# Five weight buffers for the experts, heavy and light blocks in turn, and the shared down products inside the first block

## What is computed

```python
s = sigmoid(t @ w_router);  sb = s + b_router          # 64 scores a token
... group-limited top 8 of sb -> idx, weights wk       # normalised, times 2.5
gates = sum over the chosen of wk * one_hot(idx, 64)
act    = silu(t @ w_gate_e) * (t @ w_up_e) * gates     # each expert: 1024 -> 256
routed = act @ w_down_e                                # 256 -> 1024
shared = (silu(t @ w_gate_s) * (t @ w_up_s)) @ w_down_s
y = routed + shared
```

## Time and profile before

| | |
|---|---|
| median of the timed runs | 1057.35 us |
| profiled execution, time and span | 1053.31 us, 1051.5 us |
| TensorE busy | 886.6 us (84%) |
| VectorE, ScalarE, GpSimd busy | 32%, 24%, 15% |
| DMA: bytes moved, mean rate | 299.57 MB, 285 GB/s |
| landing of a gate, up, down load, median | 11.4, 23.2, 22.4 us |
| TensorE waiting for gate/up weights at L1342 | 88.3 us |

### The profile page before, as it was taken

How to read it: one execution, slowest core, us unless ns; L and a number is a source line. 1 busy time by engine, 2 the same in 40 slices (tenths; PEclk the granted TensorE clock), 3 DMA queues, 4 the chain that set the end, 5 groups by cost and what they waited for, 6 DMA issues and landing times.

```text
span 1051.5 us, 11948 instructions
## 1 busy us (share of the span) xinstructions
PE 886.6 (84%) x4214; PEld 520.3 (49%) x4214; DVE 334.5 (32%) x819; ACT 253.4 (24%) x430; POOL 162.8 (15%) x216
## 2 busy tenths in 40 slices
PE   4799899999899898998677969878879879888860
PEld 2578686888898853543223324333324334333320
DVE  1744644656465554221101111111101111111105
ACT  2555425343333321111101111101101111111111
POOL 6200000000002321122112122122122212212112
PEclk9999899999999999998989989989989989999995
DMA  9966777211236372899999999999999999999824
GB/s 346 353 234 216 245 258 163 80 63 60 80 120 252 140 299 88 298 306 399 405 388 402 360 392 383 380 388 378 368 356 374 387 341 390 386 370 381 339 46 183
DMA packets 90346, 299.57 MB, mean 285 GB/s; under 512 B 18372, under 2 KB 40960, under 8 KB 65344
## 3 DMA queue, kind: packets, MB, share of 16 engines
q1 hardware_dynamic: 67472, 263.21, 63.8%
q0 software_dynamic: 14128, 31.27, 11.1%
q10 hardware_dynamic: 8704, 4.54, 1.8%
HBM read 287.16 MB, written 29.63 MB: 301 GB/s over the span
## 4 chain that ended last, share of the span: by engine, by line
PE 55%; DMA 33%; DVE 5%; ACT 2%; issue 2%; POOL 1%; SPq 1%; ACTq 1%; POOLq 0%; DVEq 0%
DMA gu<-in_w_up_e_dram 31%; PE bank L1342 19%; PE bank L977 6%; PE bank L979 6%; PE bank L978 6%; PE bank L1362 4%; PE bank L1005 2%; PE bank L1233 2%; PE bank L1140 1%; PE bank L1329 1%; PE bank L1046 1%; DMA chunk_raw<-in_w_ada_dram 1%; PE bank L1252 1%; DMA y_dram<-y_sb,slot_row 1%; PE bank L1072 1%
## 5 line engine op out<-in xcount | busy, mean ns | idle before, releaser
L1342 PE MATMUL bank<-gu,x_t 128*64 128x512 f32 (+1 forms) x1024 | 316.2, 665 | 89.3 <-DMA gu<-in_w_up_e_dram 88.3
L1342 PEld LDWEIGHTS bank<-gu,x_t 128*64 128x64 f32 (+1 forms) x1024 | 113.5, 166 | 260.7 <-issue 242.9
L1362 PE MATMUL bank<-dn,a_t 128*64 128x512 f32 (+1 forms) x512 | 145.3, 597 | 1.2 <-ACT y_sb L940 1.2
L646 POOL DMA_INDIRECT y_dram<-y_sb,slot_row x40 | 63.6, 1590 | 479.9 <-issue 255.5
L1781 DVE TENSOR_TENSOR act_sb<-silu_sb,bank 128x256 f32<-128x256 f32 x40 | 16.9, 421 | 363.4 <-ACT silu_sb L949 363.4
L949 ACT ACTIVATE silu_sb<-bank 128x256 f32<-128x256 f32 x40 | 15.4, 385 | 365.7 <-PE bank L1342 365.7
L977 PE MATMUL bank<-h_hi,chunk_lo 128*128 128x384 f32 x240 | 84.7, 353 | 0.0
L1362 PEld LDWEIGHTS bank<-dn,a_t 128*64 128x64 f32 (+1 forms) x512 | 48.5, 150 | 69.3 <-issue 68.0
L979 PE MATMUL bank<-h_hi,chunk_hi 128*128 128x384 f32 x240 | 80.9, 337 | 0.0
L978 PE MATMUL bank<-h_lo,chunk_hi 128*128 128x384 f32 x240 | 80.8, 337 | 0.0
L940 ACT ACTIVATE y_sb<-bank,slot_gate 128x512 f32<-128x512 f32 x80 | 50.7, 684 | 123.9 <-PE bank L1362 113.5
(11 more groups left out here) (328 smaller groups left out, 1044.4 us busy)
## 6 DMA issues: line engine op xcount, KB each, us to landing
gu<-in_w_gate_e_dram SPq DMA_DIRECT2D x64, 1024.0 KB, 11.4
gu<-in_w_up_e_dram SPq DMA_DIRECT2D x64, 1024.0 KB, 23.2
dn<-in_w_down_e_dram SPq DMA_DIRECT2D x64, 1024.0 KB, 22.4
chunk_raw<-in_w_ada_dram SPq DMA_DIRECT2D x24, 1024.0 KB, 8.8
chunk_raw<-in_w_in_dram SPq DMA_DIRECT2D x18, 1024.0 KB, 5.4
chunk_raw<-in_w_out_dram SPq DMA_DIRECT2D x4, 1024.0 KB, 4.9
chunk_raw<-in_w_pa_dram SPq DMA_DIRECT2D x2, 1024.0 KB, 4.9
chunk_raw<-in_w_pb_dram SPq DMA_DIRECT2D x2, 1024.0 KB, 5.0
```

What stands on the lines that cost most here:

```text
L646: pool.indirect_dma_start(y_dram[:, :], bass.IndirectOffsetOnAxis(ap=slot_row[:, u % UN:u % UN + 1], axis=0), y_sb[u % 2][:, :], None, bou ...
L1342: mm = pe.matmul(bank[2 + u % 2][at_x, :].rearrange("p (g n) -> p g n", g=2), x_t[:, cols], wide[:, :, k, :], start=(k == 0), stop=(k == K ...
L1362: mm = pe.matmul(bank[5 + half][at_x, :], a_t[:, cols], dn[x % RING][:, wc], start=(k == 0), stop=(k == 1))
```

## The change

- A fifth buffer. The place of the shared weights becomes buffer 4, and the new buffer 3 lies over the routing tables and over `h2_row` (24 KB for each partition from EX + 138.5). Small tables that live on are moved, and so is `shared_sb`.
- The first group runs in the order `HLHLHLHLLL`. Its H experts are at places 0, 3, 6 and 9 and are loaded first, into buffers 0, 1, 2 and 3. The fourth waits for `sides_mm` and `h2_stored` now.
- Which expert uses which buffer is a table: `SLOT0` for the first group; in the others H experts use buffer 4, and L experts take 2, 1, 3, 0 in turn.
- The three shared down products move into block 0, behind its gate and up products and the next transposes. `turn_tokens(0)` moves ahead of them and of the last activation transposes.
- VectorE's tables for further passes are made inside blocks 2 to 7 of the first group.
- At the router VectorE scales the first tile before it normalises the third, and TensorE turns all three tiles before `route(0)`.

```diff
-ORDER0, ORDER = "HHHHLLLLLL", "HLLHLHLLHL"
+ORDER0, ORDER = "HLHLHLHLLL", "HLLHLHLLHL"
-RING = 4
+RING = 5
-        ring = [EX + 84, EX, EX + 24, EX + 60]
+        ring = [EX + 84, EX, EX + 24, EX + 138.5, EX + 60]
+        def shared_turn(u, first):
+            return ((0, 1, 2),)[u] if first and u < 1 else ()
+        SLOT0 = [0, 4, 0, 1, 4, 0, 2, 1, 4, 3, 0, 2, 1, 4, 3, 0]
+        heavy_slot, light_slots = 4, (2, 1, 3, 0)
...
             def load_gu(x, group, e):
+                k, y = slot_of(x, group is None), earlier(x, group is None)
                 if group is None:
-                    if x >= RING:
-                        sp.wait_ge(S["gu_used"], x - RING + 1)
+                    if y is not None:
+                        sp.wait_ge(S["gu_used"], y + 1)
+                    elif k == RING - 1:
+                        sp.wait_ge(S["sh_mm"], TT)
...
-            sp.wait_ge(S["sh_mm"], TT)
-            load_gu(FIXED - 1, None, slice(FIXED - 1, FIXED))
+            for n, x in enumerate(FIRST_FOUR):
+                if n == FIXED - 1:
+                    sp.wait_ge(S["sides_mm"], 1)
+                    sp.wait_ge(S["h2_stored"], 16 * TT)
+                load_gu(x, None, slice(n, n + 1))
+                load_dn(x, None, slice(n, n + 1))
...
-            for u in range(FIXED, BPG):
-                now = [(x, expert_at(slice(x, x + 1))) for x in turns[True][u]]
+            for u in range(BPG):
+                now = [(x, expert_at(slice(x, x + 1))) for x in turns[True][u] if x not in FIRST_FOUR]
...
-            turn_rows2(0)
-            turn_rows2(1)
+            for t in range(TT):
+                turn_rows2(t)
             pe.wait_ge(S["router_loaded"], 16)
             route(0)
-            turn_rows2(2)
             route(1)
...
                     turn_tokens(i + 1, u + 1, first)
+                    for t in shared_turn(u, first):
+                        shared_down(t)
...
+            turn_tokens(0, 0, True)
             shared_turn_act(2)
-            for t in range(TT):
-                shared_down(t)
-            turn_tokens(0, 0, True)
             block_turn(0, True)
...
+            scale_rows(0)
             normalise2(2)
...
-            numbers(2, 2)
+            x_copy(0)
             shared_a(2)
-            x_copy(0)
```

More of the change, by code:

```diff
@@ L921, in _ @@
             shared_silu(2)
-            act.wait_ge(S["h2_stored"], 16 * TT)
-            for t in range(TT):
-                shared_out(t)
             act.wait_ge(S["passes_ready"], 1)
@@ L950, in block_turn @@
                     x_copy(i + 1)
+                    for t in shared_turn(u, first):
+                        shared_out(t)
                     if first and u == 1:
@@ L1589, in _, with scale_rows @@
             split_low(dve, number[("out", 1)])
+            def scale_rows(t):
+                cond = int(t > 0)
+                dve.wait_ge(S["xt2"], 2 * t + 1)
+                for k in range(4):
+                    ins = dve.tensor_scalar(h2_t[:, k, t * P:(t + 1) * P], bank[4 + 2 * t % 4][:, k * P:(k + 1) * P],
+                                            scale2[:, k, cond:cond + 1], mod_t[:, 3, k, cond:cond + 1], ALU.mult, ALU.add)
+                ins.then_inc(S["h2_ready"], 1)
             def normalise2(t):
@@ L1609, in _ @@
                     normalise2(n - 10)
+            scale_rows(0)
             normalise2(2)
[L1611 to L1617 removed]
+            scale_rows(1)
+            scale_rows(2)
             dve.wait_ge(S["tables_made"], 3)
@@ L1771, in _, with later_passes @@
+            def later_passes(u):
+                if u == 2:
+                    later_experts()
+                elif u == 3:
+                    later_tables(table)
+                elif u == 4:
+                    later_tables(rows)
+                elif 5 <= u < 5 + MAXPASS - 1:
+                    later_ranks(u - 4)
             passes = dve.value_load(more_i[0:1, 0:1], min_val=0, max_val=MAXPASS - 1) + 1
```

141 lines of the change are left out of this document (81 added, 60 removed).

## The result

Four runs each, taken together: the kernel before 1057.01 us (1056.22 to 1060.07), the change 1047.41 us (1045.01 to 1048.85). The ratio is 0.9902 with a 95% interval of [0.9873, 0.993], so 10 us less, 7 to 13. The forecast was 1035 us; 1047 lies inside its range and almost on the rival "the holes stay" (1046).

A forecast was written before the change was run, and what follows sets the result against it. Weight loads were taken to bound the expert stage, with DMA engines partly idle. Savings of 10 (first group) + 11 (later holes) + 1 (router) = 22 us took 1057.35 to 1035 us, range 1022 to 1049.

The forecast's parts named there:

- the holes stay: Rival: idle DMA holes from 580 us on remain, only parts 1 and 3 come; 1046 us, chance 0.15.
- What bounds the kernel: Expert stage: weight loads set the pace; full queue 395 GB/s beside gathers and adds, 381 with idle time.
- Part 1: First expert group: earlier loads and block 0 ahead of the shared downs save about 10 us, bounds 7 and 14.
- Part 2: From 580 us on: a fifth buffer deepens the queue, closing idle DMA holes; about 11 us less, bounds 0 and 18.5.
- Part 3: Router: scaling the first tile earlier hides the third tile's transposes; about 1 us less, bounds 0 and 1.7.
- the rule that the prediction quotes: First gather: a semaphore increment follows all earlier writes of its DMA engine; done about 397, with the fourth expert.
- What costs nothing: VectorE's table copies inside blocks, later shared-result stores and an unchanged number of products were claimed to add no time.
- A fuller queue is a slower queue: Rival: in the expert stage a never-ending backlog lowers the rate from 381 to 368 GB/s; 1064 us, chance 0.09.
- All comes back, by bytes: Rival: 14 + 18.5 + 1.7 = 34 us come off, loads running at 395 GB/s; 1023 us, chance 0.14.
- the prediction's own signs: Expert stage: 390 GB/s from 480 to 980 us; wrong if full queue under 385 or holes remain with five buffers.

The follow-up runs named there:

- e3: The change with SP's first-group loads reordered, loads whose buffer is free going ahead of down loads that wait: 1042.32 us, 0.9845 of the kernel before.
- e4: The change with the three shared down products put back ahead of block 0's gate and up products: 1056.33 us, 0.9974 of the kernel before.
- e1: The change with loads in groups 1 to 3 also waiting for the expert four places before, as with four buffers: 1051.39 us, 0.9925 of the kernel before.
- e7: e5 with loads in groups 1 to 3 also waiting for the expert four places before: 1039.47 us, 0.9825 of the kernel before.
- e12: e11 with loads in groups 1 to 3 also waiting for the expert four places before: 1026.17 us, 0.9687 of the kernel before.
- e14: e13 with loads in groups 1 to 3 also waiting for the expert four places before: 1008.44 us, 0.9524 of the kernel before.
- e15: The kernel before, four buffers and old SP order, with only folded token slots and swapped halves for every second heavy expert: 1028.25 us, 0.9696 of the kernel before.
- e10: The change with the router's order as before (third normalisation before first scaling, first product before third tile's transposes): 1053.03 us, 0.9941 of the kernel before.
- e16: The change with folded token slots and swapped halves, its own SP order in the first group kept: 1015.72 us, 0.9587 of the kernel before.
- e13: e11 with every second heavy expert in groups 1 to 3 filling the upper 64 slots first: 1008.08 us, 0.9521 of the kernel before.
- e2: The change with an expert's tokens spread over its 64 slots in eighths (rank i + 8j in slot 8i + j): 1060.39 us, 1.0009 of the kernel before.
- e5: The change with sixteen tokens filling every second slot of 32 and the next sixteen those between: 1036.18 us, 0.9794 of the kernel before.
- e9: The change with slots as in e5 but folded, the second sixteen ranks placed from the other end: 1031.24 us, 0.9745 of the kernel before.
- e11: The change with the folded slots of e9 and SP's first-group order of e3 together: 1023.25 us, 0.9661 of the kernel before.

## Why the prediction was wrong

The direction was right, and so was the first half of the working; 1035 us needed three parts, and one of them was not there.

- **What bounds the kernel.** Right that the loads do and that the rate of a full queue is 395 GB/s or more. Wrong in reading "one minus the share" as time in which the queue was short. It was time in which some engines were.
- **Part 1, 10 us.** Right in its steps; the table below has them. The gap behind block 4 came out at 5.8 us (one minus the share, 472 to 484 us in windows of 2 us) instead of 3.9. e3, which closes it and issues places 4 and 5 sooner, gives 6. The move of the shared products, the reason for half of the step, is measured by e4 as 7.6 us, give or take 3. The lead by loads is 11 us behind that gap, though in this pair of executions the mixer ended 1.1 us later in the change (first load issued at 358.89 against 357.75).

| us | forecast | change |
|---|---|---|
| three loads issued | 388.5 | 387.55 |
| block 0's products | 403 | 402.14 |
| two down loads wait from | 425 | 423.46 |
| block 1's products | 426 | 423.65 |
| five loads go by | 437.8 | 438 |
| next down loads; place 7 | 450; 450 | 446.9; 449.1 |
| block 3's products | 454 | 455.3 |
| place 8 | 459 | 465.0 |
| block 4's products | 466.5 | 469.4 |

- **Part 2, 11 us. This is the step that failed:** "I expect nearly all of the 12.3 us to go and take 11." None of the 12.3 us went: the holes sum to 14 us in the change. e1 measures the fifth buffer behind the first group at 2.4 us, e7 at 3.3, e12 at 2.9, e14 at 0.4, each give or take 3 or so; together they allow some 2 us, not 11. The lower bound given was 0, "if the holes come from SP's order alone"; the end of the range was right and its reason was not. The step took an idle share of the engines for a queue that had run short. From 580 us on the cause is the drift of the engines: e15 closes the holes of the kernel before (399 GB/s at 1.02 instead of 375 at 0.98) with four buffers and its old SP order. The clue could have been read beforehand: cut into windows of 2 us, the hole of the earlier trace rows at 780 us shows 0.71, 0.44 and 0.44 and never 0, though SP had issued nothing for 10 us. Where the queue did run short, at 426 to 436 us of the change, the share went from 0.98 to 0.39, 0.03 and 0.00.
- **Part 3, 1 us.** The sign is right and the size short. The traces show 2.9 us against the kernel before where 1.7 were counted, because the sum left out the granted clock; e10's timed runs say 4 us, give or take 3.5. The first gather did not take any of it back: issued at 388.41, it landed at 397.2, 8.8 us later, while TensorE came to the transposes that need it at 399.35. The median of the earlier trace rows gave 400.5 and the rule that the prediction quotes 397. The fourth expert's gate and up weights landed at 396.4 and its down weights at 399.9, so the trace agrees with that rule's time, and with its "when the fourth expert is" for the first two loads only.
- **What costs nothing.** Nothing contradicts it: block 1 starts on time with VectorE's tables behind it, and e16 has the 11 us of parts 1 and 3 in full, give or take 3. No run took these tables away by themselves.
- **The rivals.** "The holes stay" came true in number (1046 against 1047.4), with a cause other than the down loads that it named. "A fuller queue is a slower queue" fell: 399 GB/s over 360 us in e13 and e15. "All comes back, by bytes" did come back, to 1015.72 in e16 and below, but by the slots and not by the buffer. Of the prediction's own signs, 374 GB/s over 580 to 940 us and holes with five buffers were the two that spoke against it.

That 1047 lies so near "the holes stay" is no luck in the number, since parts 1 and 3 are what came; the reason given for that rival was another. It is shown by e2, e5, e9, e13 and e15 that the filling of the slots sets the marks and the pace, and by e1, e7, e12 and e14 that the depth is worth little either way. It is only argued that the adds and the gathers share this cost in some proportion; no run took one of them away.

## What to carry to other kernels

A share of DMA time below 1 over several microseconds, with loads still queued, was no short queue here. Look at how far the 16 marks of one load lie apart before adding a buffer. If they lie much further apart than one load takes, look for a transfer that does not fill all its partitions (a gather with empty slots), and spread what it fills: here over all groups of four partitions within each 32, from both ends of a group's order in turn, and over both halves of 64 in turn. Loads that wait in one line do cost their full wait while the engines are together, as they did in the first group here; there SP's order was worth 6 to 7 us and moving TensorE's work off the first buffer 5 to 8. A short wait can also cost clock: at the router the granted clock fell behind a wait of 2.4 us and not behind one of 1.1, which was another microsecond in 48 products.

## What was not expected of the hardware

- The parts of one 1 MB load are done up to 14 us apart on average (13.6 in the kernel before), though a load takes 2.5 us of a full queue. The distance is 2 us ahead of the expert stage and adds up over some 200 us of it. The Trainium skill ("DMA: Bandwidth & Descriptors", Why a DMA increments its semaphore by 16 and not by 1) says that each of 16 engines reports its own part and that only the full count means landed; the marks agree, and 14 us is what it comes to here.
- As far as the marks tell, the rows of a gather or an add by indices go to the engines by the partition of the slot, in groups of four slots that repeat after 32, and by halves of 64: four groups of four marks in e2, two groups of eight in e9 and e11, no groups in e13.
- With the engines even, one core takes in 399 to 401 GB/s over 360 us, weights, gathers and adds together (e13, e15, e16), where 374 looked like a bound.
